# A one-core transformer kernel on Trainium2: modulation sums, gates, roots of the norms and the memory values moved

## What is computed

```python
mod = silu(c) @ ada_w + ada_b                      # 6 vectors of 1024
sh1, sc1, g1, sh2, sc2, g2 = split(mod, 6)
h = modulate(rms_norm(x, norm1_g), sh1, sc1)       # h * (1 + sc1) + sh1
z = h @ w_in + b_in                                # ..., ga, gb are its last 2 x 1024 columns
...
merged = sigmoid(ga) * (ym @ p_mlstm) + sigmoid(gb) * (ya @ p_moba)
x = x + g1 * (merged @ w_out)
h = modulate(rms_norm(x, norm2_g), sh2, sc2)
x = x + g2 * ((silu(h @ w_gate) * (h @ w_up)) @ w_down)
x = rms_norm(x, normf_g)
# second block: even layer (short convolution and pooling mixer), odd layer (DSA and HGRN2);
# in each: x = x + mixer(norm(x)); x = x + cross_attention(norm(x), norm(mem)); x = x + peer(norm(x))
```

## Time and profile before

| | |
|---|---|
| median of 3 runs | 2699.72 us (2695.72 to 2700.98) |
| the profiled execution, its own time | 2697.7 us |
| its span in the profile | 2695.4 us |
| PE busy | 2131.8 us (79%) |
| DVE busy | 1393.7 us (52%) |
| POOL busy | 1140.1 us (42%) |
| ACT busy | 729.3 us (27%) |
| mean granted clock of PE | 0.905 |

### The profile page before, as it was taken

One profiled execution on the slowest core, in us unless ns is written; L12 is line 12 of the kernel. 1 busy time (PEld: TensorE's weight loads), 2 busy tenths in 40 slices (PEclk: granted clock), 3 DMA queues, 4 the chain that ended last, 5 costly groups with the idle time before them and its releaser, 6 DMA issues. The chain is left out here.

```text
span 2695.4 us, 23784 instructions
## 1 busy us (share of the span) xinstructions
PE 2131.8 (79%) x8566; PEld 1389.6 (52%) x8566; DVE 1393.7 (52%) x2971; ACT 729.3 (27%) x1348; POOL 1140.1 (42%) x809
## 2 busy tenths in 40 slices
PE   4898979989688488887878869858785777868776
PEld 4755679878577344333333348847672333323332
DVE  6353231135525877755455534672378776455554
ACT  2323245454334111111111135233431111211112
POOL 3602467887446333332333337214362333333331
PEclk9999989999788799898999889978897989999998
DMA  8455445555334699998999955113337999999996
GB/s 323 148 171 173 156 152 169 171 172 181 109 98 145 234 425 424 413 421 366 408 421 426 422 213 181 61 49 108 109 120 317 426 426 426 423 388 426 426 426 265
DMA packets 126934, 735.58 MB, mean 273 GB/s; under 512 B 14264, under 2 KB 14264, under 8 KB 60512
## 3 DMA queue, kind: packets, MB, share of 16 engines
q0 software_dynamic: 77600, 555.18, 49.6%
q1 hardware_dynamic: 49072, 178.83, 20.0%
q10 hardware_dynamic: 144, 0.05, 0.0%
HBM read 732.94 MB, written 1.06 MB: 272 GB/s over the span
## 5 line engine op out<-in xcount | busy, mean ns | idle before, releaser
L579 POOL TENSOR_TENSOR W_lo<-W,W_hi 128x1024 fp32r<-128x1024 f32 x264 | 643.2, 2443 | 439.1 <-ACT W_hi L1143 438.2
L800 PE MATMUL banks<-arena 128*128 128x512 f32 x912 | 443.8, 636 | 144.0 <-ACT arena L1199 143.8
L800 PE MATMUL banks<-rows_b,arena 128*128 128x512 f32 x684 | 346.8, 655 | 123.2 <-ACT arena L1199 123.2
L1143 ACT ACTIVATE W_hi<-W 128x1024 fp32r<-128x1024 f32 x264 | 276.7, 1058 | 464.3 <-PE banks L714 386.5
L800 PEld LDWEIGHTS banks<-arena 128*128 128x128 f32 x912 | 180.2, 203 | 397.0 <-issue 255.1
L2032 DVE SCALAR_TENSOR_TENSOR arena<-arena,banks 128x1024 f32<-128x1024 f32 x228 | 276.3, 1220 | 197.7 <-DMA arena<-in_uv,p_eid 196.5
L636 POOL DMA_INDIRECT arena<-in_uv,p_eid x228 | 213.9, 938 | 377.3 <-PE banks L800 368.7
L714 PE MATMUL banks<-HT_hi,W_hi 128*128 128x256 f32 x1128 | 333.5, 296 | 43.7 <-POOL W_lo L579 20.4
L714 PE MATMUL banks<-HT_hi,W_lo 128*128 128x256 f32 x1128 | 330.4, 293 | 0.0
L714 PE MATMUL banks<-HT_lo,W_hi 128*128 128x256 f32 x1128 | 330.1, 293 | 0.0
L1193 ACT ACTIVATE arena<-arena 128x4 f32<-128x4 f32 x128 | 26.3, 205 | 1055.6 <-DVE arena L2036 1055.5
(11 more groups left out here) (267 smaller groups left out, 2663.6 us busy)
## 6 DMA issues: line engine op xcount, KB each, us to landing
W<-in_weights SPq DMA_DIRECT2D x336, 512.0 KB, 3.6
gain<-in_rows POOLq DMA_DIRECT2D x10, 512.0 KB, 5.8
arena<-in_uv,p_eid POOLq DMA_INDIRECT x228, 10.9
rows_b<-in_uv,p_eid POOLq DMA_INDIRECT x171, 10.8
arena<-in_rows POOLq DMA_DIRECT2D x1, 2048.0 KB, 17.2
arena<-in_keys POOLq DMA_DIRECT2D x2, 1024.0 KB, 5.0
arena<-bias_scratch POOLq DMA_DIRECT2D x2, 1024.0 KB, 7.8
rows_c<-in_uv,p_eid POOLq DMA_INDIRECT x113, 10.6
```

Source lines behind the costliest of these rows:

```text
L579: po.tensor_tensor(W_lo[:, slot, :], W[:, (PARTS * n + part) % RAW_RING, :], W_hi[:, slot, :].bitcast(F32), ALU.subtract).then_inc(S_("lo_ ...
L800: mm = pe.matmul(sums[c], diag[:, n % DIAGS, :], rows[slot][:, D + c * BLK:D + (c + 1) * BLK], start=j == 0, stop=j == SEL - 1)
L1143: act.activation(W_hi[:, q % SPLIT_RING, :], wait_landed(act, n, part), ACT.Copy).then_inc(S_("hi_made"), 1)
```

## The change

Five things are changed.

1. **Head.** DVE sums ada tiles 0 and 2 only. PE takes tiles 1 and 3 with `ada_columns`: the weights as the stationary side and one column of silu(c) as the moving side, 32 products of 128x1 in a tile. POOL's loads of small tables start when the first 6 parts have been summed.
2. **Modulation and gates.** The four gate tiles (`gate0` to `gate3`) are multiplied in the attention, half a tile (two parts) after each of eight units, into two held banks; the ACT copies and POOL subtractions for them lie there too. Of the other ada tiles, 4 and 5 stay on PE in the "a" units, 6 to 9 are summed on DVE in the merge, 10 and 11 on DVE in FF; one 128x512 product with ones adds the partitions of each (`ada_total`).
3. **Roots.** `rstd` is now 12 small DVE operations (an initial guess from the bits and three Newton steps), once for both token tiles. ACT only squares. No Ln or Exp is left in a norm.
4. **Memory.** The memory's transposes are split once, inside FF, into areas of their own, `M_hi` and `M_lo`. `x_k0` follows `down` at once. The first value tile (`x_v0`) runs after `e_pool`, the second (`x_w0`) after `e_out`.
5. `e_out`'s ACT copies all follow the split of `e_yT`; the order of the weights in memory and in SP's loads follows the new order of use.

The diff, cut to its core:

```diff
-ADA_IN_M = {0: [4], 1: [5], 2: [6], 3: [7]}
-ADA_IN_A = {0: [8], 2: [9], 4: [10], 6: [11]}
+GATES_IN_M = {0: (0, 0), 1: (0, 2), 2: (1, 0), 3: (1, 2)}
+GATES_IN_A = {0: (2, 0), 1: (2, 2), 4: (3, 0), 5: (3, 2)}
+ADA_IN_A = {2: [4], 6: [5]}
+ADA_IN_FF = {2: 10, 4: 11}
+ADA_OUT_FF = {4: 10, 6: 11}
...
+    t += [("gate0", 0), ("gate1", 0), ("gate2", 0), ("ada4", 0), ("gate3", 0), ("ada5", 0)]
+    t += [("merge", 3), ("ada6", 0), ("ada7", 0), ("merge", 7), ("ada8", 0), ("ada9", 0)]
...
+            def gate(n, first):
...
+                    q = parts_before(tile_no[f"gate{n}"]) + part
+                    pe.wait_ge(S_("lo_made"), q + 1)
...
+                        bank = banks[:, plan.bank("gate", t), :]
+                        for j in range(2):
+                            for m, (w, a) in enumerate(((hi, HT_hi), (lo, HT_hi), (hi, HT_lo))):
+                                mm = pe.matmul(bank, a[:, 2 * part + j, t * P:(t + 1) * P], w[:, j, :],
...
+            def ada_total(i):
+                pe.wait_ge(S_("ada_summed"), PARTS * (i - 3))
+                pe.matmul(claim(f"ada{i}"), ones, ada_acc[i], start=True, stop=True).then_inc(pe_filled, 1)
...
+            def ada_columns(i):
+                bank = banks[:, plan.bank("ada"), :]
+                for part in range(PARTS):
+                    w = raw(i, part)
+                    for j in range(2):
+                        k = 2 * part + j
+                        for b in range(4):
+                            mm = pe.matmul(bank[:, 4 * i + b:4 * i + b + 1], w[:, j, b * P:(b + 1) * P], stat(620 + k, 1),
...
+            ada_columns(1)
             pe.wait_ge(S_("const_in"), 16)
             norm_T(0)
+            ada_columns(3)
...
+            natural("x_v0", 1, halves=(M_hi, M_lo))
             after(pe, "e_pool", 1)
             pe.wait_ge(S_("e_split"), 2)
             natural("e_out", 2)
+            natural("x_w0", 1, halves=(M_hi, M_lo))
...
+            high_gates(0, 3)
             m_units = [(p, t) for p in range(2) for t in range(NT)]
...
+            def rstd(sums, out, width):
+                n = sums.shape[-1]
+                x, y = stat(480, n), stat(488, n)
+                ts(x, sums, 1.0 / width, ALU.mult, EPS, ALU.add)
+                step(v.tensor_copy(y, x.bitcast(U32)))
+                ts(out.bitcast(U32), y, -0.5, ALU.mult, float(0x5F3759DF), ALU.add)
+                for _ in range(3):
+                    tt(y, out, out, ALU.mult)
+                    stt(y, y, -0.5, x, ALU.mult, ALU.mult)
+                    stt(out, y, 1.5, out, ALU.add, ALU.mult)
...
             for c in range(2):
+                sum_ada(6 + 2 * c)
+                sum_ada(7 + 2 * c)
                 v.wait_ge(S_("gate_ready"), c + 1)
...
             split_T("mg_T")
+            for i in range(6, 10):
+                take_ada(f"ada{i}", 0, i)
...
             for i in range(NF // 2):
+                if i in ADA_IN_FF:
+                    sum_ada(ADA_IN_FF[i])
                 after(v, f"ff_g{i}")
                 bank = filled(v, f"ff_u{i}")
```

More of the change, by code:

```diff
@@ L176, in make_plan @@
     p.add("m_g1")
-    units_of(p, "m", 4, ADA_IN_M)
+    p.add("gate", 2, marks=0, hold=True)
+    units_of(p, "m", 4)
     p.add("m_pv", NT)
     units_of(p, "a", 8, ADA_IN_A)
+    p.release("gate")
     p.add("a_pv", NT)
     p.add("y_T", 4)
-    p.add("merge", 16)
+    p.add("merge", 8)
     p.add("mg_T", 4)
+    for i in range(6, 10):
+        p.add(f"ada{i}")
     p.add("w_out", 4)
@@ L196, in make_plan @@
     p.add("e_pool", 2)
+    p.add("x_v0", 2)
     p.add("e_out", 4)
+    p.add("x_w0", 2)
     for l in range(2):
@@ L272, in is_split @@
 def is_split(stage, i):
-    return not (stage.startswith("ada") or stage in ("x_k1", "x_v1") or stage == "merge" and i % 8 == 7)
+    return not (stage.startswith("ada") or stage in ("x_k1", "x_v1", "merge"))
 def build(nc, io):
@@ L753, in natural @@
+            def natural(stage, n_tiles, act=None, halves=(HT_hi, HT_lo)):
                 for n in range(n_tiles):
-                    product(first + n, [(stage, at + 2 * n + t, [(slice(0, BLK), slice(0, BLK), cols_at(t * P, P), False)])
-                                        for t in range(NT)], act)
-            def attend(name, units, scores, n_keys, base, between={}):
+                    product(tile_no[stage] + n, [(stage, 2 * n + t, [(slice(0, BLK), slice(0, BLK), cols_at(t * P, P), False)])
+                                                 for t in range(NT)], act, halves=halves)
@@ L766, in attend @@
                         score(u + 2)
-                    for i in between.get(u, ()):
-                        pe.wait_ge(S_("c_ready"), 1)
-                        ada(i)
+                    between(u)
                     if base is None:
@@ L1235, in _, with high_gates @@
             step(act.activation(stat(32, 8), stat(32, 8), ACT.Ln, bias=1.0), "log1p_ready")
+            gate_parts = [(n, part) for n in range(4) for part in range(PARTS)]
+            def high_gates(first, end):
+                for n, part in gate_parts[first:end]:
+                    high(f"gate{n}", part, part + 1)
+            high_gates(0, 3)
             m_units = [(p, t) for p in range(2) for t in range(NT)]
@@ L1310, in _ @@
                 high("e_z", i=i)
-            high("e_out", 0, 2)
+            high("x_v0")
             act.wait_ge(pe_filled, plan.mark("e_z", 7))
@@ L2096, in _ @@
                 norm(5 + 3 * l, X, gain_of(5 + 3 * l))
+                if l == 0:
+                    for t in range(NT):
+                        bank = filled(v, "x_w0", t)
+                        step.free(v.tensor_copy(x_vs[0][:, t, BLK:], bank), "x_w0", t)
                 split_T(f"T{5 + 3 * l}")
```

289 lines of the change are left out of this document (172 added, 117 removed).

## The result

The changed kernel takes 2708.62 us (median of 12 runs, 2702.68 to 2714.03); the kernel before, run beside it, 2699.59 us (12 runs, 2692.06 to 2704.22). The ratio is 1.0041, with a 95% interval of 1.0031 to 1.0051: slower by 9 us by the medians and 11 by the ratio, where 12 us less were forecast. The profiled execution took 2708.08 us, its span 2705.8.

A forecast was written before the change was run, and what follows sets the result against it. Outside the gathers, PE was taken as busiest in some 750 us, with DVE's new operations priced by POOL. Terms 11 + 8 - 17 - 1 + 5 - 29 + 11 + 0 = -12 gave 2685.7 us profiled, 2688 median; range 2655 to 2713.

The forecast's parts named there:

- first step: Whole kernel: work leaving PE and ACT costs DVE 0.2 or 2.4 us an operation, by what POOL does.
- head's term: Head: PE's 64 column products at 0.214 us a record make the first `z_qk` product 11 us later; range -3 to +14.
- hm's term: Attention, root of hm: two ACT table loads go, 12 small operations come; -1 us.
- memory stage's term: `down`'s end to `e_z`: value tiles leave, norms 3 and 4 then bound; -29 us, bounds -35 to -18.
- Rotary products, +7: Attention: three low halves of the gates' input fall beside the second set of rotary products and slow them; +7 us.
- mLSTM units -6, MoBA units +8: Attention: "m" units swap four ada tiles for four half gate tiles, -6; "a" units get four halves, net two ada tiles fewer, +8.
- Merge, -17: Merge: PE loses four gate tiles, DVE gains four sums with 20 us of ring-place waits; -17 us, bounds -22 to -13.
- FF, +5: FF: norm 2's stall goes, two DVE sums come at 25 us a tile, mostly covered; +5 us, bounds -3 to +30.
- slow rival: FF: DVE's sums and norm 2 delay the taking of banks, PE stops; +30, total 2713 us; chance 0.20.
- fourth rival: Value tiles don't gain: half of the Newton operations meet POOL, memory stage gives -18, total 2699 us; chance 0.15.
- `e_z` to `x_q0`, +11: After `e_z`: moved value tiles only partly fit PE's idle time; +5 to `e_out`, +6 on to `x_q0`; bounds +2 to +17.
- Other norms, 0: Seven more roots: two gain 2 to 2.6 us each, others lose 1 to 2; 0 us, bounds -12 to +4.

## Why the prediction was wrong

Its first step, that DVE's operations cost 0.2 or 2.4 us by what POOL does, stands as far as it goes: one low half holds an operation for some 2.4 us, but two or three in a row held one for 5 or 7. Three steps failed. The head's term put nothing on POOL's earlier loads (5.5 us); hm's term left out POOL's queue behind the row buffer (6.2); and the memory stage's term was too small by 8.4, most of it roots at 16.0 us where 9.6 were put. Together they are 20 of the 22 us between forecast and result. Point by point:

- **Head, +11: 5.5 short.** With the loads held back `z_qk` began exactly 11.0 later, but that is luck in part. The sum put the start of the columns at 17.4, the transposes at 2.0 and the totals at 1.9; in that run they were 14.2, 3.4 and 3.6. PE took the parts of ada 1 as they landed and had no turn of DVE's to wait for, and 8 products are 16 records, at the price of the earlier trace rows 3.4 us and not 1.9. The errors cancel to 0.2 us. The columns' own price was right, 0.214 a record. The step that failed is one that the forecast did not take: the same edit moved POOL's loads of 5.4 MB ahead of ada 3's parts. The change's own list says so, and no price was set on it.
- **Rotary products, +7:** +7.1, of which 5.7 went away when the three low halves were moved.
- **mLSTM units -6, MoBA units +8:** -4.2 (from 30.6 to 26.4 between the first unit's scores and the last products) and +8.4.
- **hm, -1: measured +5.2.** Failed. The term counted the root and not the queue: POOL's program has a wait between gate 1 and gate 2, three low halves gather behind it, and they run as a block beside the chain to the MoBA units. "Beside one low half, 2.4 us" was the wrong size: one operation was held for three.
- **Merge, -17: -14.5.** The waits for ring places, put at 20, were 20.3 (11.47 and 8.82). The rest of DVE's part took 3 us more, 1.2 of it shorter waits for parts.
- **FF, +5: +5.6.** The number is right and its working isn't. The sums took 15.1 and 8.0 us, not 25 each, and PE stood still once for 7.56 us, for a ring place and not for a bank. The slow rival, at 0.20 the one that would have given the sign, did not happen; the sign came from elsewhere.
- **Memory stage, -29: -20.6.** That norms 3 and 4 bound was right, the size off. The two roots were put at 4.8 each, with one operation held; they took 6.6, with two held, and 9.4, with two held for three low halves. That is 6.4 of the 8.4 missing. The products and squares took 2.0 more (two products at 4.58 for 2.6), the part from norm 4 to `e_z` 1.6 more (5.1 for 3.5), while the additions and the wait behind them took 1.6 less. The fourth rival named this at -18, but set it against a sum that was else right. And there was a second bound close by that no term looked at: PE was done with the keys 34.3 us after `down`'s end, and in the run with ACT's roots `e_z` came 4.4 us behind them. By these two numbers `e_z` could not have come sooner than some 38.7 us after `down` (an estimate), where 36 was forecast.
- **`e_z` to `x_q0`, +11: +14.8**, 6.9 where 5 was put, and 7.9 where 6 was.
- **Other norms, 0:** the part behind `x_q0` is 5.2 shorter, within what near-identical kernels differ by. What it holds for the roots stays open; with all roots on ACT it was 1943.0, with Newton 1944.1.

Most places where DVE got work beside POOL were priced too low. With the upper ends of four terms (head +14, attention +9, merge -13, memory -18) and the rest as forecast, the sum is +7, near the +10 measured. That it comes so near is luck too: the head (+16.5) and the attention (+16.1) lay outside even these ends, the merge and the memory stage inside. None of the prediction's own signs of being wrong came up: FF was under 150 us, `z_qk` not before 50, and the small operations did meet low halves. A sign for a head beyond 62 and one for `e_z` were lacking.

## What to carry to other kernels

When work moves between engines, follow every wait that moves with it, and on the queue that no term speaks of too: here POOL's wait for a row buffer and its loads cost 5 us each. A stream that a slower reader empties holds its ring places longer, and the next reader of the ring pays for it. And where small operations of one engine are held by long ones of another, take the number of held operations from a row with the same neighbours, not from a lone one; a chain of 12 gives 12 chances to be held.

## What the runs showed of the hardware

- One DVE product of 128x8, 0.17 us alone, took 6.95 us beside three POOL subtractions that ran back to back in 7.01. Two DVE operations of 128x2 took 5.40 us beside two subtractions in a row. At the second set of rotary products the two engines took turns: four products in 7.00 and two additions in 3.44 us, beside three subtractions in 7.84. So a DVE operation can be passed over by more than one POOL operation.
- Products of 128x1 came 0.214 us a record both where the profile's granted clock reads 1.00 and where it reads 0.52. The Trainium skill (TensorE: Matmul & The Clock Gate, section LDWEIGHTS) gives 107 ns for a load of 128 columns; no stretch of these columns showed it.
- With the roots as 12 small operations on DVE or with four ACT table loads in each norm, the stages were nearly as long. From the changed kernel to the one with all roots on ACT, the head is 0.4 us shorter, `w_out` with norm 1 0.9 longer, FF with norm 2 3.2 shorter, the memory stage 0.9 shorter and `e_out` with norm 5 2.3 longer (untouched stages differ by up to 1.6). The chain of norms 3 and 4 by itself, with POOL at work beside it, was 39.4 us by the small operations and 32.8 by the table loads; in the head, with POOL idle, a root's 12 operations took 2.3 us.
